# Scores of the second mixers as three float32r products of high and low parts, in row halves

## The reference, cut to what matters

```
q_n, kc, vc, ks, vs, kw, vw, gates, q_r, k_r, v_r, g_r = split(h @ w_in)
s_c = q . kc_compressed  * scale - slopes * (t - c_mid)     # 32 compressed keys
s_s = q . ks             * scale - slopes * dist            # selected branch
s_w = q . kw             * scale - slopes * dist            # window branch
o = g0 * softmax(s_c) vc' + g1 * softmax(s_s) vs + g2 * softmax(s_w) vw
```

## Time and profile before

| | |
|---|---|
| median of three runs | 3144.71 us |
| the profiled execution | 3143.91 us |
| its span, first to last instruction | 3142.6 us |
| PE busy | 3101.2 us (99%) |
| DVE / ACT / POOL busy | 1359.0 / 1220.8 / 1348.1 us |
| PE matmul instructions | 16832 |

### The profile page before, as it was taken

The page is one execution under the profiler, slowest core; times in us unless marked ns, Lnnn a source line. Parts: engine busy times, 40 slices in busy tenths (PEclk is TensorE's granted clock), DMA queues, the critical chain, the costliest instruction groups (busy, mean ns, idle before and its releaser), DMA issues.

```text
span 3142.6 us, 42608 instructions
## 1 busy us (share of the span) xinstructions
PE 3101.2 (99%) x16832; PEld 2602.6 (83%) x16832; DVE 1359.0 (43%) x2491; ACT 1220.8 (39%) x2100; POOL 1348.1 (43%) x871
## 2 busy tenths in 40 slices
PE   8999999999999999999999999999999999999998
PEld 6877888898888987878888889888897778798887
DVE  7676533114330355755443304332056665363311
ACT  5456322233222345664432223322344564442221
POOL 4452444443444453462344444444534354334443
PEclk9999999999999999999999999999999999999999
DMA  4221333332333242231233332333432132223332
GB/s 163 81 68 54 91 97 101 95 114 67 98 100 101 78 142 62 74 112 44 81 91 97 98 90 88 101 94 101 119 97 88 48 101 82 80 69 100 101 95 67
DMA packets 80933, 285.15 MB, mean 91 GB/s; under 512 B 8928, under 2 KB 11360, under 8 KB 80480
## 3 DMA queue, kind: packets, MB, share of 16 engines
q1 hardware_dynamic: 79728, 278.59, 29.7%
q10 hardware_dynamic: 1008, 3.84, 0.3%
HBM read 280.30 MB, written 2.10 MB: 90 GB/s over the span
## 4 chain that ended last, share of the span: by engine, by line
PE 90%; DVE 4%; POOL 2%; issue 2%; ACT 2%; DMA 1%; ACTq 0%; DVEq 0%; POOLq 0%
PE bank L269 23%; PE bank L271 23%; PE bank L270 23%; PE bank L277 4%; PE bank L278 4%; PE bank L279 4%; POOL wlo L263 2%; PE bank L1524 2%; PE bank L1494 1%; PE bank L1508 1%; PE bank L3547 1%; PE bank L3573 1%; PE bank L603 1%; ACT whi L249 1%; DMA raw<-wstream 0%
## 5 line engine op out<-in xcount | busy, mean ns | idle before, releaser
L263 POOL TENSOR_TENSOR wlo<-raw,whi 128x256 fp32r<-128x256 f32 (+3 forms) x787 | 1229.3, 1577 | 1413.6 <-ACT whi L249 1380.7
L269 PE MATMUL bank<-hhi,whi 128*128 128x512 f32 x2080 | 821.4, 395 | 12.7 <-DVE wlo L263 11.0
L270 PE MATMUL bank<-hlo,whi 128*128 128x512 f32 x2110 | 821.9, 390 | 0.0
L271 PE MATMUL bank<-hhi,wlo 128*128 128x512 f32 x2080 | 810.6, 390 | 0.0
L249 ACT ACTIVATE whi<-raw 128x1024 fp32r<-128x1024 f32 (+2 forms) x502 | 501.7, 1031 | 362.3 <-PE bank L271 292.2
L269 PEld LDWEIGHTS bank<-hhi,whi 128*128 128x128 f32 x2080 | 391.1, 188 | 98.0 <-issue 19.3
L270 PEld LDWEIGHTS bank<-hlo,whi 128*128 128x128 f32 x2110 | 396.8, 188 | 81.2 <-issue 1.4
L271 PEld LDWEIGHTS bank<-hhi,wlo 128*128 128x128 f32 x2080 | 390.7, 188 | 82.5
L269 PE MATMUL bank<-ff_ahi,whi 128*128 128x512 f32 x660 | 256.7, 389 | 0.0
L271 PE MATMUL bank<-ff_ahi,wlo 128*128 128x512 f32 x660 | 256.7, 389 | 0.0
L270 PE MATMUL bank<-ff_alo,whi 128*128 128x512 f32 x630 | 245.1, 389 | 0.0
(11 more groups left out here) (429 smaller groups left out, 5211.7 us busy)
## 6 DMA issues: line engine op xcount, KB each, us to landing
raw<-wstream SPq DMA_DIRECT2D x508, 512.0 KB, 3.5
raw<-wstream SPq DMA_DIRECT2D x20, 256.0 KB, 2.6
xa_v<-memT ACTq DMA_DIRECT2D x2, 1024.0 KB, 4.9
outT<-x SPq DMA_DIRECT2D x4, 512.0 KB, 2.8
raw<-wstream SPq DMA_DIRECT2D x4, 420.0 KB, 4.3
x<-xT ACTq DMA_DIRECT2D x2, 512.0 KB, 7.9
x<-xT SPq DMA_DIRECT2D x2, 512.0 KB, 8.1
consts<-consts SPq DMA_DIRECT2D x1, 1004.0 KB, 7.5
```

Of the source, the lines that this page charges most:

```text
L263: last = g.tensor_tensor(h.lo[:, o:o + step], h.raw[:, o:o + step], h.hi[:, o:o + step].bitcast(F32), ALU.subtract)
L269: t.matmul(out, l[0], r[0], start=start, stop=False)
L270: t.matmul(out, l[0], r[1], start=False, stop=False)
L271: return t.matmul(out, l[1], r[0], start=False, stop=stop)
```

## The change

Queries, keys and compressed keys are split into high and low parts, and each score product becomes three float32r products that add up in PSUM, still in pairs of row halves. For that:

- DVE writes queries to the scratch tiles `tmp` 0 to 3. ACT makes the high parts `m_qhi` from them, DVE the low parts `m_qlo`. The same is done for the keys (`m_khi`, `m_klo`) with `tmp` 0 and 1, which may be written again once the low parts of the queries are made.
- The compressed keys get a high part (ACT) and a low part (DVE, from PSUM).
- `m_klo` lies in room that the memory's keys need later, so ACT copies it once during the attention (two copies of 128x512); PE waits for that copy from a fixed unit on (`MOVED`).
- Scratch squares of the memory go to `m_gr` in place of `xa_k`.
- PE waits for the low parts of keys and compressed keys before the attention.

The diff, cut to its core:

```diff
+WHOLE, SPLIT = ((0, 0),), ((0, 0), (0, 1), (1, 0))
@@ Attention.pe_scores
             for h in range(heads):
-                for b in range(2):
-                    u = self.units[step + b]
-                    last = t.matmul(k.bank[b][:, h * 32:(h + 1) * 32], u["q"][h], u["k"], start=True, stop=True, skip_group_check=True)
+                for l, (qs, ks) in enumerate(SPLIT):
+                    for b in range(2):
+                        u = self.units[step + b]
+                        last = t.matmul(k.bank[b][:, h * 32:(h + 1) * 32], u["q"][qs][h], u["k"][ks], start=l == 0, stop=l == len(SPLIT) - 1,
+                                        skip_group_check=True)
...
         for n in range(len(both[0])):
-            for parts in both:
-                p, to = parts[n]
-                last = t.matmul(to, p["q"], p["k"], start=True, stop=True, skip_group_check=True)
+            passes = both[0][n][0]["passes"]
+            for l, (qs, ks) in enumerate(passes):
+                for parts in both:
+                    p, to = parts[n]
+                    last = t.matmul(to, p["q"][qs], p["k"][ks], start=l == 0, stop=l == len(passes) - 1, skip_group_check=True)
@@ MixerTwo.pe
+        t.wait_ge(*self.k_lo[1])
+        t.wait_ge(*self.kc_kept[0])
         self.att.pe(...)
@@ MixerTwo.act
             weight_hi(k, [self.uch, self.keych][kv].c + 2)
+        for n in range(4):
+            a.activation(self.qhi[:, n * T:(n + 1) * T], k.tmp[n][:, :], ACT.Copy).then_inc(self.q_hi.sem)
         weight_hi(k, self.cch[0][0].c + 2)
+        for n in range(2):
+            a.wait_ge(*self.k_kept[n])
+            a.activation(self.khi[:, n * T:(n + 1) * T], k.tmp[n][:, :], ACT.Copy).then_inc(self.k_hi.sem)
         self.act_hidden(0)
...
+        a.wait_ge(*self.grch[1].done[-1])
+        for n in range(2):
+            o = slice(n * T, (n + 1) * T)
+            last = a.activation(self.klo[1][:, o], self.klo[0][:, o].bitcast(F32), ACT.Copy)
+        last.then_inc(self.klo_moved.sem)
@@ MixerTwo.dve
         for c, ch in enumerate(self.qch):
-            run(keep_dve(k, ch, lambda m: self.qT[:, (2 * c + m) * T:(2 * c + m + 1) * T], DH ** -0.5, self.q_kept))
+            run(keep_dve(k, ch, lambda m: k.tmp[2 * c + m][:, :], DH ** -0.5, self.q_kept))
...
+        for n in range(4):
+            self.dve_low(n, self.q_hi[n], self.qhi, self.qlo, self.q_lo)
         for n in range(2):
             v.wait_ge(*self.keych.done[n])
-            v.tensor_tensor(self.keys[n][:, :], k.bank[4 + n][:, :], k.row[:, :], ALU.mult).then_inc(self.k_kept.sem)
+            v.wait_ge(*self.q_lo[n])
+            v.tensor_tensor(k.tmp[n][:, :], k.bank[4 + n][:, :], k.row[:, :], ALU.mult).then_inc(self.k_kept.sem)
+        for n in range(2):
+            self.dve_low(n, self.k_hi[n], self.khi, self.klo[0], self.k_lo)
         for ch in self.cch[0]:
             weight_lo(k, ch.c + 2, e=v)
         self.dve_hidden(0)
+        v.wait_ge(*self.kc_hi[0])
+        v.scalar_tensor_tensor(self.kcmp_lo[:, :], k.bank[0][:, 384:384 + DH], 0.5, self.kcmp_hi[:, :].bitcast(F32), ALU.mult,
+                               ALU.subtract).then_inc(self.kc_kept.sem)
+
+    def dve_low(self, n, hi_made, hi, lo, made):
+        v, o = self.k.nc.vector, slice(n * T, (n + 1) * T)
+        v.wait_ge(*hi_made)
+        v.tensor_tensor(lo[:, o], self.k.tmp[n][:, :], hi[:, o].bitcast(F32), ALU.subtract).then_inc(made.sem)
```

More of the change, by code:

```diff
@@ L1480, in pe_scores @@
                 t.wait_ge(*self.free[b])
+        if "wait" in self.units[step]:
+            t.wait_ge(*self.units[step]["wait"])
         if step in self.several:
@@ L1491, in pe_scores @@
         for n in range(len(both[0])):
-            for parts in both:
-                p, to = parts[n]
-                last = t.matmul(to, p["q"], p["k"], start=True, stop=True, skip_group_check=True)
-                if n == len(parts) - 1:
-                    last.then_inc(self.scores.sem)
+            passes = both[0][n][0]["passes"]
[3 more added lines that the diff above has]
+                    last = t.matmul(to, p["q"][qs], p["k"][ks], start=l == 0, stop=l == len(passes) - 1, skip_group_check=True)
+                    if n == len(parts) - 1 and l == len(passes) - 1:
+                        last.then_inc(self.scores.sem)
     def pe_turn(self, i):
@@ L2806, in __init__ @@
         self.at_keys = put.at[0]
-        self.both_keys = put("m2_ksw", 2 * T)
-        self.keys = [self.both_keys[:, n * T:(n + 1) * T] for n in range(2)]
+        self.khi = put("m2_khi", 2 * T, F32R)
         at_vr = put.at[0]
@@ L2856, in __init__ @@
         self.at_weights = put.at[0]
-        units, self.rows = [], []
+        units, self.rows, at = [], [], 0
         for qb in range(TB):
@@ L2867, in __init__ @@
                     for gi in range(2):
-                        parts = [self.score_part(qb, j, gi, branches) for j in js]
+                        moved = at >= self.MOVED
+                        parts = [self.score_part(qb, j, gi, branches, self.klo[moved]) for j in js]
                         units.append(dict(n=sum(p["n"] * len(branches) for p in parts), parts=parts))
+                        if moved:
+                            units[-1]["wait"] = self.klo_moved[0]
                     self.rows.append((qb, js, branches))
+                    at += sum(self.per_row(len(units) - 2 + gi, qb) for gi in range(2))
         self.cat_nsa = NormOutputs(k, 4, self.up[:, :], self.o_dump, self.total[:, :], lambda j: k.p2(l, "nsa_out_g", j),
@@ L2965, in pe, with score_part @@
         self.out.pe(2)
-    def score_part(self, qb, j, gi, branches):
+    def score_part(self, qb, j, gi, branches, klo):
         n, rows, o = (qb + 1) * P, slice(DH * gi, DH * gi + DH), j * T + qb * P
-        keys = self.both_keys[rows, :].rearrange("p (b t) -> p b t", b=2)[:, :, 0:n] if len(branches) == 2 else self.keys[branches[0]][rows, 0:n]
-        return dict(n=n, q=self.qT[rows, o:o + P], k=keys, slope=SLOPES[4 * gi + j], dist=self.k.c("dist", T - n, n), at=j * P,
+        both = [x[rows, :].rearrange("p (b t) -> p b t", b=2)[:, :, 0:n] if len(branches) == 2 else x[rows, branches[0] * T:branches[0] * T + n]
+                for x in (self.khi, klo)]
+        return dict(n=n, q=[x[rows, o:o + P] for x in (self.qhi, self.qlo)], k=both, passes=SPLIT, slope=SLOPES[4 * gi + j],
+                    dist=self.k.c("dist", T - n, n), at=j * P,
                     v=[lambda kb, at=br * P + gi * DH: self.vtok[:, kb * 256 + at:kb * 256 + at + DH] for br in branches])
```

38 lines of the change are left out of this document (24 added, 14 removed).

## The result

The changed kernel takes 3153.97 us (median of eight runs, 3152.66 to 3154.32); the kernel before, on the same chip, 3144.7 us. The ratio is 1.0029, with a 95% interval of 1.0019 to 1.0038: slower by 9.3 us. The prediction was 3150.3 us, range 3145.5 to 3158. The profiled execution has a span of 3153.0 us against 3142.6. One execution of a later kernel, that of experiment 6, took 10590.98 us, for which no row gives a reason; its median is 3143.71 us with it and 3143.56 without.

What follows compares the result with a forecast made beforehand. PE was taken to bound the attention, a chain of POOL and DVE splits and a weight load the opening. Scores -1.7 and opening +4.5 gave +2.8 us a layer, +5.6 in both: 3150.3 us, range 3145.5 to 3158.

Steps and rivals of the forecast that it cites:

- What bounds the kernel: Whole chain: PE is 90% of the time that sets the end; DVE has room in the attention, none in the opening.
- The scores on PE: Attention: float32r groups of 256 to 512 columns get cheaper, compressed groups dearer; sum -1.7 us a layer.
- rival 3: Score groups on PE: later passes of a half don't hide weight loads, 5 us a layer; 3160.3 us, chance 0.13.
- rival 4: Score groups on PE: the 0.2 us edge goes, -5.2 us a layer; 3139.9 us, chance 0.07.
- rival 3's last case: Score groups: float32r pairs don't run side by side at all, some 17 us more a layer, 3188; outside the range.
- The opening: Splits on DVE, ACT and POOL delay DVE's first weight split 4.9 us; PE stands 4.2 us; +4.5 us a layer.
- what the empty queue gives back: Opening, loads of the values' weights: starting on an empty queue returns 0.4 us, bounds 0 and 1.2.
- rival 1: Opening: DVE's subtractions don't lose turns to POOL, so +0.5 us a layer; 3145.7 us, chance 0.18.
- The clock while PE stands: Openings: PE's clock might fall during the stand above 4 us, +3 us in all; left out of the sum.
- The copies of `m_klo`: ACT in the attention: 1.1 us of copies, bounds 0 and 1.1 us a layer, taken as 0.
- rival 2: Openings: PE's clock falls while it stands, +3 us in all; 3153.3 us, chance 0.12.
- the signs that the prediction named for being wrong: Stand under 3 or over 6 us, groups off by 0.05 us, clock leaving 1.00, or new wait behind `m_klo` copies.

Runs made afterwards that it cites:

- experiment 6: Changed kernel with query and key splits moved behind DVE's four weight splits, and ACT's two low-key copies behind the weight split they preceded; 3143.71 us.
- the products alone: Changed kernel without the splits: three float32r products per score, all on the same unsplit operands; 3140.46 us, ratio 0.9988 to the kernel before.
- experiment 4: Changed kernel plus three unused fp32 matmuls of 512 columns per layer, placed where PE stands in the opening; 3150.44 us, ratio 1.0020 to the kernel before.
- experiment 3: Changed kernel, but the four subtractions for the queries' low parts read their first operand from PSUM, not SBUF; 3145.62 us, ratio 1.0004 to the kernel before.
- the splits alone: Changed kernel with all splits, waits and copies, but each score is one fp32 product on the high parts; 3157.47 us, ratio 1.0041 to the kernel before.

## Why the prediction was right, and what it missed

The forecast was slower by 5.6 us, and 9.3 came. The direction and the range held and the largest term was right, but two terms that I had put at nothing took more than half of the net loss. By its steps, for two layers (measured in lateness, which sums to 9.8 in the profiled execution where the medians give 9.3):

- **What bounds the kernel.** Right for PE's own work and for DVE's work in the opening. That DVE and ACT have room in the attention was right for DVE's list and wrong for ACT's (the copies, below).
- **The scores on PE**, -3.4 us. Right: each group within 0.04 us, and the products alone gained 3.9 in the attentions. The difference is two compressed groups in each layer that stand ahead of a wait. Rivals 3 (loads not hidden) and 4 (edges vanish) are refuted: two later passes of 512 columns follow at 0.23 us each, and the edge of 0.2 stays. That a pair in row halves costs one full product was taken from fp32 rows that do not show a full product; experiment 4 has one (three full fp32 products in 2.6 us, 0.86 each, as the pair), so the step was sound. The some 17 us a layer of rival 3's last case come to 18.7 by its own terms, which is what its 3188 uses, and the 3.5 us a layer of rival 4 hold only with rival 1 beside it.
- **The opening**, +9.0 us. Without the clock 4.30 + 4.24 = 8.5 us, which experiment 4 shows. The working holds row by row: the second low part held by POOL (2.9 us, "some 3"), DVE's first weight split at 1124.45 for 1124.2, in an execution whose shared instructions run 0.6 us late from the start. ACT's first split for the second half of `cch[0]` came 0.7 us late, which I had not listed; it moved a part of the stand ahead of it, 3.84 us in place of 4.2. (The upper bound of what the empty queue gives back was mis-stated: a stand of 4.2 less a wait of 0.9 leaves 3.3 us and not 4.9 - 1.2; 4.3 came.) The turns were 5.2 of the 8.5, as experiment 3 shows, and rival 1 is refuted.
- **The clock while PE stands**, 0 in my sum. This is the step that failed: I made it a rival at 0.12 because the only fall I could read was at the program's start. It came in both layers and took 3.4 us in the profiled execution. The price per fall that I read there, 1.5 us, was near for layer 0 (1.3) and low for layer 1 (2.2).
- **The copies of `m_klo`**, 0 to 2.2 us, taken at 0. The second step that failed: 0.8 us a layer, 1.7 in all. I argued from the waits of PE on ACT, of which there were none in the earlier trace rows. The copies delay ACT's list, DVE waits for ACT, PE for DVE, and that wait was in the earlier trace rows, 1.5 us on DVE's scaling. "PE never waits for ACT" holds only for the last link, and only for layer 0: in layer 1 of the kernel before PE waits once for ACT's `att_p`, 0.7 us.

The sum -3.9 + 8.5 + 3.4 + 1.7 = 9.7 us is close to the 9.8 measured. Two of the signs that the prediction named for being wrong came true, the clock and the wait behind the copies. What came is rival 2 (3153.3 us, chance 0.12) with the copies' price on top of it; my own number, 3150.3, missed by 3.7. That the total stayed in the range owes something to luck: the range had room for the clock, and the 1.0 us that the groups and the opening came out below my terms took off more than half of the copies' price.

## What to carry to other kernels

Before you add a DVE operation that reads two SBUF tiles, find out what POOL does at that moment: six of them in each of two layers cost 12 us in one place, 3.4 us of it through the clock, and 1.2 at most in another; in the bad place, moving one operand of four of the six to PSUM left 3.4 us. When a change makes TensorE stand for some microseconds, read the granted clock behind the stand and add the price of half clock. When you call work on an engine hidden, follow its list through the engine that waits for it. And before you explain a microsecond of one trace, see how far that execution lies from the median.

## What the runs showed of the hardware that I had not expected

- In all four places where TensorE stood for 3.84 us (two layers of the changed kernel and of the splits alone) its clock was at 1.2 GHz behind the stand, for 14 to 24 matmuls of 256 columns, which cost 1.1 to 2.2 us. Behind stands of 1.6 us (low parts from PSUM) and 1.3 us (behind 2.7 us of filler) it stayed at 2.4 GHz. Three useless products in each layer's stand made the kernel 3.5 us faster.
- A float32r pair in row halves costs 0.11 us for 32 and for 64 columns.
- In the attention, 0.43 us more on PE cost nothing ahead of the smaller of the two waits for DVE's scaling in the earlier trace rows, 0.5 us: of four equal additions a layer only two showed in full.
